# Some low-half subtractions on GpSimd, a 256-column first update of x, and more places between VectorE's instructions

## The reference

```python
for l in range(DEPTH):
    u = rms_norm_2(h, norm_pre_mix[l])
    p = (u @ w_in[l]).astype(jnp.float32)
    p_ret, p_hgrn, p_ml, p_rw = split_cols_2(p, GROUP_COLS)
    ...                       # retention, hgrn2, mlstm, rwkv7: four recurrences, width 512 each
    mixed = jnp.concatenate([o_ret, o_hgrn, o_ml, o_rw], axis=-1).astype(h.dtype) @ w_out[l]
    h = h + rms_norm_2(mixed, norm_post_mix[l])
    u = rms_norm_2(h, norm_pre_ffn[l])
    ffn = (jax.nn.silu(u @ w_ffn_gate[l]) * (u @ w_ffn_up[l])) @ w_ffn_down[l]
    h = h + rms_norm_2(ffn, norm_post_ffn[l])
```

## Time and profile before

| | us |
|---|---|
| median of 3 runs | 3925.11 |
| lowest, highest | 3915.49, 3926.25 |
| the profiled execution | 3918.05 |
| its span, first to last instruction | 3916.7 |
| granted clock of TensorE, mean of the span | 0.984 |
| busy: TensorE, VectorE, ScalarE, GpSimd | 3797.8, 2255.0, 1794.1, 104.3 |
| subtractions of low halves, line 527 | 1176, busy 1393.8 |

### The profile page before, as it was taken

The page is one execution under the profiler, slowest core; times in us unless marked ns, Lnnn a source line. Parts: engine busy times, 40 slices in busy tenths (PEclk is TensorE's granted clock), DMA queues, the critical chain, the costliest instruction groups (busy, mean ns, idle before and its releaser), DMA issues.

```text
span 3916.7 us, 49184 instructions
## 1 busy us (share of the span) xinstructions
PE 3797.8 (97%) x19948; PEld 3203.5 (82%) x19948; DVE 2255.0 (58%) x3526; ACT 1794.1 (46%) x2519; POOL 104.3 (3%) x61
## 2 busy tenths in 40 slices
PE   8999999999999999989999999999999989999998
PEld 7886778787898897778888888888988778888887
DVE  5665666675555746764454444566656664445444
ACT  6454545445454424444444444545325454444443
POOL 0000000000010000000000000010000000000000
PEclk9999999999999999999999999999999999999999
DMA  7655546563554405446666655544225446666654
GB/s 239 183 168 146 145 135 178 158 188 101 182 165 134 122 26 159 146 145 190 191 188 189 201 194 193 172 127 146 63 72 153 156 140 189 190 191 189 201 194 169
DMA packets 341427, 628.34 MB, mean 160 GB/s; under 512 B 21089, under 2 KB 63025, under 8 KB 340433
## 3 DMA queue, kind: packets, MB, share of 16 engines
q1 hardware_dynamic: 331920, 611.53, 51.4%
q10 hardware_dynamic: 9280, 13.69, 1.0%
HBM read 623.04 MB, written 2.10 MB: 160 GB/s over the span
## 4 chain that ended last, share of the span: by engine, by line
PE 88%; DVE 6%; ACT 3%; POOL 1%; issue 1%; DMA 1%; SPq 0%; ACTq 0%; DVEq 0%; POOLq 0%
PE bank L621 74%; DVE weights_low L527 2%; PE bank L745 2%; PE bank L1301 1%; PE bank L1398 1%; PE bank L2499 1%; PE bank L2513 1%; PE bank L2106 1%; PE bank L2512 1%; ACT weights_high L514 1%; PE bank L600 1%; PE bank L1381 1%; POOL stat L706 1%; PE bank L1304 0%; POOL arena L706 0%
## 5 line engine op out<-in xcount | busy, mean ns | idle before, releaser
L527 DVE TENSOR_TENSOR weights_low<-weights,weights_high 128x1024 fp32r<-128x1024 f32 (+3 forms) x1176 | 1393.8, 1195 | 980.6 <-ACT weights_high L514 969.1
L514 ACT ACTIVATE weights_high<-weights 128x1024 fp32r<-128x1024 f32 (+3 forms) x1176 | 1205.8, 1030 | 1345.2 <-PE bank L621 1289.6
L621 PE MATMUL bank<-weights_high,x_high 128*128 128x512 f32 (+3 forms) x2816 | 1117.1, 397 | 22.2 <-DVE weights_low L527 12.0
L621 PE MATMUL bank<-weights_low,x_high 128*128 128x512 f32 (+3 forms) x2816 | 1086.3, 386 | 0.0
L621 PE MATMUL bank<-weights_high,x_low 128*128 128x512 f32 (+3 forms) x2816 | 1085.9, 386 | 0.0
L621 PEld LDWEIGHTS bank<-weights_high,x_high 128*128 128x128 f32 x2816 | 535.8, 190 | 136.2 <-DVE weights_low L527 19.5
L621 PEld LDWEIGHTS bank<-weights_low,x_high 128*128 128x128 f32 x2816 | 534.7, 190 | 102.4
L621 PEld LDWEIGHTS bank<-weights_high,x_low 128*128 128x128 f32 x2816 | 536.3, 190 | 93.0
L621 PE MATMUL bank<-x_high,weights_high 128*128 128x256 f32 x960 | 279.6, 291 | 12.7 <-DVE arena L650 6.0
L621 PE MATMUL bank<-weights_high,ff_high 128*128 128x512 f32 x704 | 274.1, 389 | 0.0
L621 PE MATMUL bank<-weights_low,ff_high 128*128 128x512 f32 x704 | 273.9, 389 | 0.0
(11 more groups left out here) (381 smaller groups left out, 3613.4 us busy)
## 6 DMA issues: line engine op xcount, KB each, us to landing
weights<-in_w_in_dram SPq DMA_DIRECT2D x208, 512.0 KB, 3.6
weights<-in_w_ffn_gate_dram SPq DMA_DIRECT2D x176, 512.0 KB, 3.7
weights<-in_w_ffn_up_dram SPq DMA_DIRECT2D x176, 512.0 KB, 3.7
weights<-in_w_ffn_down_dram SPq DMA_DIRECT2D x176, 512.0 KB, 3.6
weights<-in_w_out_dram SPq DMA_DIRECT2D x128, 512.0 KB, 3.6
weights<-in_even_w_in_dram SPq DMA_DIRECT2D x88, 512.0 KB, 3.6
weights<-in_odd_w_in_dram SPq DMA_DIRECT2D x80, 512.0 KB, 3.7
weights<-in_mem_w_kv_dram SPq DMA_DIRECT2D x32, 512.0 KB, 4.0
```

What stands on the lines that cost most here:

```text
L514: self.high_mark[g] = self.high_split.count(act.ran(nc.scalar.activation(high, raw, ACT.Copy)), act.clock)
L527: self.low_mark[g] = self.low_split.count(dve.ran(nc.vector.tensor_tensor(low, raw, high.bitcast(F32), ALU.subtract)), dve.clock)
L621: ins = pe.ran(nc.tensor.matmul(out, l, r, start=(u + c + x + y == 0), stop=(u == blk.n - 1 and c == UNIT - 1 and y == 1)))
```

## The change

It has four parts. `lows` compares the planner's clocks and hands a subtraction to GpSimd where GpSimd would be done, by a reckoned 3.0 us, before VectorE would be (VectorE's clock or the high half's time, plus 1.2), and before the unit is used (2.5 us for each unit that is still ahead). `post_norm` updates x's first tile in two halves of 256 columns, turns its first two chunks with the new `turn_first` in two banks, with a mark for each chunk, and issues the last tile's gain multiplication (`times_gain(3)`) behind that turn instead of ahead of the sum. The recurrences yield in more places. The reciprocal of rwkv is cut into four of 256 columns.

```diff
@@ lows @@
             raw, high, low = self.raw[g % RAW][:, :, 0:w], self.w_high[g % HIGH][:, :, 0:w], self.w_low[g % RAW][:, :, 0:w]
+            begin, last = expected_at([self.high_mark[g]]), self.pe.clock + (g - self.g) * 2.5
+            if max(pool.clock, begin) + 3.0 < min(max(dve.clock, begin) + 1.2, last):
+                pool.wait_ge(self.high_mark[g])
+                self.low_mark[g] = self.low_split_pool.count(
+                    pool.ran(nc.gpsimd.tensor_tensor(low, raw, high.bitcast(F32), ALU.subtract)), pool.clock)
+                self.no_low.pop(0)
+                continue
             dve.wait_ge(self.high_mark[g])
@@ new @@
+    def turn_first(self, AT, c, src, gain):
+
+        nc, pe, act, dve = self.nc, self.pe, self.act, self.dve
+        turned = []
+        for j in range(2):
+            pe.wait_ge(*self.bank_free[4 + j])
+            for t in range(T):
+                ins = pe.ran(nc.tensor.transpose(self.ps[4 + j][:, t * P:(t + 1) * P], src(c + j, t), self.c("ident")))
+            turned.append(pe.did(ins))
+        copied = []
+        for j in range(2):
+            act.wait_ge(turned[j])
+            copied.append(act.did(nc.scalar.activation(AT.high[:, c + j, :], self.ps[4 + j][:, 0:S], ACT.Copy, scale=gain[:, c + j:c + j + 1])))
+        for j in range(2):
+            dve.wait_ge(copied[j])
+            AT.ready[c + j] = self.bank_free[4 + j] = [dve.did(nc.vector.scalar_tensor_tensor(
+                AT.low[:, c + j, :], self.ps[4 + j][:, 0:S], gain[:, c + j:c + j + 1], AT.high[:, c + j, :].bitcast(F32),
+                ALU.mult, ALU.subtract))]
@@ post_norm @@
-        if "out" in name:
-            self.times_gain(3)
         self.rms_of(self.squares, rs)
...
-        def update(nb):
-            cut = slice(nb * TILE, (nb + 1) * TILE)
+        def update(nb, lo=0, hi=TILE):
+            cut = slice(nb * TILE + lo, nb * TILE + hi)
...
-        marks = {0: update(0)}
+        marks = {}
+        marks[0] = update(0, 0, 2 * P)
         for c in range(0, KC, 2):
             nb = c // 4
-            yield [marks[nb]]
-            pe.wait_ge(marks[nb])
-            self.turn(AT, c, self.x_chunk, 4 + c // 2 % 4, gain)
+            yield [marks[c]]
+            pe.wait_ge(marks[c])
+            if c == 0:
+                self.turn_first(AT, c, self.x_chunk, gain)
+            else:
+                self.turn(AT, c, self.x_chunk, 4 + (c // 2 + 1) % 4, gain)
+            if c == 0:
+                marks[2] = update(0, 2 * P, TILE)
+                if "out" in name:
+                    self.times_gain(3)
             if c % 4 == 0 and nb < 3:
-                marks[nb + 1] = update(nb + 1)
+                marks[c + 4] = marks[c + 6] = update(nb + 1)
@@ cumulate @@
             dve.did(nc.vector.tensor_tensor_scan(out[:, k:k + width], one, src[:, k:k + width], 0.0, ALU.mult, ALU.add))
+            if k // width % 2:
+                yield
@@ rwkv, prologue @@
         dve.wait_ge(m)
         dve.seq(nc.vector.tensor_scalar(sq, sq, 1e-12, None, ALU.max))
-        dve.seq(nc.vector.reciprocal(sq, sq))
-        yield
+        yield
+        for c in range(4):
+            dve.did(nc.vector.reciprocal(sq[:, c * S:(c + 1) * S], sq[:, c * S:(c + 1) * S]))
+            yield
+        dve.wait_ge(dve.now())
         dve.seq(nc.vector.tensor_tensor(kk, kk, sq, ALU.mult))
+        yield
         dve.did(nc.vector.tensor_tensor(a, a, kk, ALU.mult))
```

More of the change, by code:

```diff
@@ L332, in build @@
             self.low_split = Counter(sem("low_split"))
+            self.low_split_pool = Counter(sem("low_split_pool"))
             self.unit_used = Counter(sem("unit_used"))
@@ L517, in lows @@
     def lows(self, least=-1):
-        nc, dve = self.nc, self.dve
+        nc, dve, pool = self.nc, self.dve, self.pool
         while self.no_low:
@@ L1853, in post_norm @@
         acc = self.acc_mix if "out" in name else self.acc_down
-        def update(nb):
-            cut = slice(nb * TILE, (nb + 1) * TILE)
+        def update(nb, lo=0, hi=TILE):
+            cut = slice(nb * TILE + lo, nb * TILE + hi)
             for t in range(T):
                 xv = self.x[:, t, cut]
-                m = dve.did(nc.vector.scalar_tensor_tensor(xv, acc[nb][:, t, :], rs.cols[:, t:t + 1], xv, ALU.mult, ALU.add))
+                m = dve.did(nc.vector.scalar_tensor_tensor(xv, acc[nb][:, t, lo:hi], rs.cols[:, t:t + 1], xv, ALU.mult, ALU.add))
                 if nxt is None:
@@ L1867, in post_norm @@
             return
-        marks = {0: update(0)}
+        marks = {}
+        marks[0] = update(0, 0, 2 * P)
         for c in range(0, KC, 2):
             nb = c // 4
-            yield [marks[nb]]
-            pe.wait_ge(marks[nb])
-            self.turn(AT, c, self.x_chunk, 4 + c // 2 % 4, gain)
+            yield [marks[c]]
[8 more added lines that the diff above has]
+                    self.times_gain(3)
             if c % 4 == 0 and nb < 3:
-                marks[nb + 1] = update(nb + 1)
+                marks[c + 4] = marks[c + 6] = update(nb + 1)
             if c % 4 == 2:
-                act.wait_ge(marks[nb])
+                act.wait_ge(marks[c])
                 for t in range(T):
@@ L2064, in hgrn @@
         yield
-        self.cumulate(cum, f, P)
+        yield from self.cumulate(cum, f, P)
         yield
@@ L2121, in hgrn @@
         exponents(1)
-        merge(-1, self.c("ident"))
-        yield
+        yield from merge(-1, self.c("ident"))
         dve.wait_ge(landed)
         for lev in range(LEVELS):
-            scale(lev)
+            yield from scale(lev)
             yield
@@ L2134, in hgrn @@
             dve.wait_ge(dve.now())
-            merge(lev, masks[:, lev, 1, :])
+            yield from merge(lev, masks[:, lev, 1, :])
         c3, E3, d3 = v3(cum), v3(E0), v3(mixed[1])
@@ L2355, in rwkv @@
         dve.wait_ge(m)
-        self.cumulate(L_, lw, P)
+        yield from self.cumulate(L_, lw, P)
         yield
```

## The result

The changed kernel takes **3982.17 us** (median of 4 runs, 3981.36 to 3986.05), the kernel before 3920.47 us beside it; the ratio is 1.0158 [1.0145, 1.0171]. The change makes the kernel 1.6% slower. I had said 3904 us and faster; the measured time lies outside the range.

What follows compares the result with a forecast made beforehand. TensorE's own work was taken to bound the kernel, VectorE mattering only where late. 8.4 + 15.4 + 6.8 - 7 - 4 + 2 - 0.6 = 21 us off the median 3925.11 gives 3904 us; range 3882 to 3928.

Steps and rivals of the forecast that it cites:

- What bounds the kernel: TensorE's own work, busy 97%; VectorE matters only where late: waits of 22.2, 19.0, 10.0 and 5.8 us.
- Layer ends, 8.4 us: Two mixer ends and the down projection: 7.5 us saved directly, 1.0 given back, 1.9 of clock gained.
- what is late next: Behind three layer ends, moved VectorE work delays low halves of chunks 2 and 3: 1.0 us given back in all.
- The 1.9 us of clock: At the three layer ends, shorter TensorE stalls were to regain 27% of about 7 us, range 0 to 5.
- Long runs, 15.4 us: Recurrences: new yields, cut reciprocal and GpSimd hand-over shorten TensorE's waits behind long VectorE runs; range 0 to 17 us.
- What I took back for it, 7 us: Recurrence chain: removed stalls let the stream run out earlier; a third of 22.2 us returned, range 0 to 17.
- My first rival: Handed back at the chain's end: recurrences, not stalls, set the stages' ends; 3915 us, chance 18%.
- The clock, +6.8 us: Beside the recurrences' removed stalls, TensorE's clock was to rise and gain 6.8 us, range -3 to 13.
- GpSimd's subtractions, 4 us lost: About 100 subtractions handed to GpSimd; blocking of two-input VectorE work costs TensorE 4 us, range 0 to 25.
- the 38 us: VectorE's loss from 50 handed-over subtractions beside two-input instructions, 0.76 us each; a tenth was to reach TensorE.
- Attention, 2 us gained: Attention stages: VectorE's inputs come from PSUM and ends wait for it; 2 us gained, range -4 to 6.
- The read port, 12%, 3947 us: Nearly all 100 handed-over subtractions meet two-input VectorE instructions, one in four delays reaches TensorE: 47 us lost; chance 12%.

Runs made afterwards that it cites:

- the fills: Kernel before plus only the hand-over, each handed-over subtraction replaced by two full-width GpSimd fills that write only, low halves left zero: 3877.80 us, ratio 0.9897.

## Why the prediction was wrong, point by point

- **What bounds the kernel**: right. The four waits are still the ones that move.
- **Layer ends, 8.4 us**: the direct part was right (7.5 us foretold; 2.9 + 1.3 + 2.9 = 7.1 measured with the ends alone). The term that failed is "I take 1.0 in all" for what is late next: 2.2 and 1.7 us came back at the two mixers. I let the low halves of chunks 2 and 3 come 4.4 us behind those of chunk 1; they came 7.6 us behind (1731.37 to 1738.95), since TensorE issued their transposes only behind the first unit's twelve matmuls. The 1.9 us of clock did not come. Total 3.8 us.
- **Long runs, 15.4 us**: the stalls do go (14.7 us of them, the 2.83 us included that I had left to GpSimd). What I took back for it, 7 us, was 16.6 us of idle time. My first rival was right in kind and too mild: it set the stalls' worth at zero, and with the places it is below zero by 17 us. Its counter-argument, a single wait of 5.8 us, was no argument: the chain was near the edge in both layers, and its slack was not in the table of waits.
- **The clock, +6.8 us**: the sign was wrong. With the places alone the bare chain's end runs at 0.50 for 31 us, and TensorE's busy time is 4.8 us longer (3802.6); in the changed kernel it is 34 us longer.
- **GpSimd's subtractions, 4 us lost**: the step that failed; the term alone measured 71.7 us lost and would have turned the forecast. The count (100 taken, 112 measured) and the price (0.19 us freed in the mean taken, by half and half; about 0.1 measured, 1.2 freed and 1.08 blocked) were near. Wrong was "of which I let a tenth reach TensorE". Between reads and writes by the same rule lie 119.7 us of VectorE and 112 us of time (71.7 slower than before against 40.6 faster), over nine tenths. That is a ratio of two totals and not a block followed through: of the 105 us between the two traces 69 are idle time of TensorE and 36 are the same matmuls at a lower clock. And the 38 us of which the tenth was taken had already been netted with what a hand-over frees; the fills show that this freed time was itself worth 40.6 us where nothing blocks. A likely reason for the high share is the rule's own condition, that VectorE's queue is behind and TensorE's use is near; a mean over the kernel does not hold for a set chosen by that. No run chose its units otherwise (the hand-over at the reciprocal keeps the condition), so this stays an argument.
- **Attention, 2 us gained**: wrong. I took VectorE's inputs there to be PSUM; the products of L1129 have two SBUF inputs, 62 of them went from 31.2 to 51.5 us, and 36 us were lost before the first recurrence.
- **What would show it**: x's update at about 13 us (14.5 came), GpSimd with 60 to 150 subtractions of 1.9 to 3 us (112 at 2.61) and no long wait behind the reciprocal held. The first waits at line 650 should halve and went from 10.0 to 12.9 us; TensorE's share should rise and fell to 96%. The sign named for "wrong", new waits for VectorE's chain operations, came: three for the products, 5.8 us in all, and two for the end of rwkv, 9.9 us; they are longer than the 1 to 2 us named. The sign of the first rival, a longer wait for the retention's end, did not come.
- **The read port, 12%, 3947 us**: the right mechanism, undersized and given too little. It was charged with one in four blocks reaching TensorE, and 25 us of gains elsewhere that did not exist.

The products in both traces, the kernel before and the changed one:

```profile
L1129 DVE TENSOR_TENSOR arena<-arena 128x256 f32<-128x256 f32 (+3 forms) x62 | 31.2, 532 | 23.1 <-POOL arena L706 22.9
```

```profile
L1156 DVE TENSOR_TENSOR arena<-arena 128x256 f32<-128x256 f32 (+3 forms) x62 | 51.5, 865 | 23.1 <-POOL arena L714 22.9
```

## What to carry to other kernels

Before work is handed to GpSimd, look at what VectorE runs in that moment, not at how idle GpSimd is: beside VectorE's two-input work a reading GpSimd instruction freed 1.2 us and took back 1.1, beside the reciprocal it was free, and beside a one-input multiplication it was not. Work that is moved only where an engine is late may be on the path by that very choice; price it at its full cost until a run says otherwise. And a visible stall taken out of one of two interleaved chains is a gain only if the other chain's slack, which no table of waits shows, can bear it: two such places, aimed at 11.9 us of stalls (3.41, 3.83 and 4.67), made the kernel 27 us slower.

## What was unexpected of the hardware

- The block can starve GpSimd: a subtraction that takes 1.9 us alone took 12.23 us beside VectorE instructions that followed each other without a gap, and none of these was longer than usual until the last.
- Most of the block fell on VectorE's other two-input work. Between fills and reads its subtractions, over half of its busy time, grew by 24 of the 119 us; those of 1024 columns took 1.244 us in the mean after, 1.229 before.
- GpSimd's fills ran at 0.91 us for 1024 columns and left VectorE's two-input instructions at their length, but not its multiplications by a constant (0.41 to 1.12 us).
